# Attends of both pairs of heads of a group of queries in one visit of the matrix engine

## The reference

```python
proj = jnp.einsum('bld,dn->bln', x, w_in) + b_in
qa, fa, ia, za, qb, kb, vb, zb, qi, ki, wi, ga, gb = jnp.split(proj, cuts, axis=-1)
oa = hgrn2_mix(qa, fa, ia, lb)                      # branch A: gated linear recurrence, 4 heads
ob = dsa_mix(qb, kb, vb, qi, ki, wi, rel_bias)      # branch B: attention over chosen keys, 8 heads of 64
...
merged = jax.nn.sigmoid(ga) * ua + jax.nn.sigmoid(gb) * ub
y = jnp.einsum('bld,de->ble', merged, w_out)
return layer_norm(ALPHA * x + y, ln_g, ln_b)
```

```python
logits = jnp.einsum('bthd,btkhd->bhtk', qh, ks).astype(f32) * (HEAD_DIM_B ** -0.5)
logits = logits + bias.transpose(0, 3, 1, 2)
logits = jnp.where(valid[:, None], logits, -jnp.inf)
p = jax.nn.softmax(logits, axis=-1)
o = jnp.einsum('bhtk,btkhd->bthd', p.astype(vs.dtype), vs)
```

## Time and profile before

| | |
|---|---|
| median of 3 runs | 471.39 us (471.04 to 473.29) |
| the profiled execution's own time | 471.07 us |
| its span, first to last instruction | 469.3 us |
| TensorE busy, share | 458.8 us, 98% |
| VectorE, ScalarE, GpSimd busy | 281.2, 217.5, 162.2 us |
| granted TensorE clock, mean | 0.997 of full speed |
| records on TensorE | 2970 matmuls |
| attends (line 635) | 160 records, 12.3 us busy |
| transposes of turns (line 620) | 80 records, 12.1 us busy |

### The profile page before, as it was taken

The page is one execution under the profiler, slowest core; times in us unless marked ns, Lnnn a source line. Parts: engine busy times, 40 slices in busy tenths (PEclk is TensorE's granted clock), DMA queues, the critical chain, the costliest instruction groups (busy, mean ns, idle before and its releaser), DMA issues.

```text
span 469.3 us, 7633 instructions
## 1 busy us (share of the span) xinstructions
PE 458.8 (98%) x2970; PEld 362.9 (77%) x2970; DVE 281.2 (60%) x542; ACT 217.5 (46%) x369; POOL 162.2 (35%) x161
## 2 busy tenths in 40 slices
PE   8999999999999999999999899999999999999994
PEld 7778888888777777666887687787888888888883
DVE  4446589999994243334999984972442332562286
ACT  5635454341336444274966656825872233342000
POOL 0444442491249722582004000000044444994000
PEclk9999999999999999999999999999999999999998
DMA  8818112243022410202022220222033332275022
GB/s 270 271 40 291 57 63 91 89 162 108 0 91 91 125 56 1 91 0 91 3 95 84 91 92 2 92 91 91 0 108 125 106 111 89 91 234 215 0 89 91
DMA packets 15876, 45.64 MB, mean 97 GB/s; under 512 B 2232, under 2 KB 3808, under 8 KB 15840
## 3 DMA queue, kind: packets, MB, share of 16 engines
q1 hardware_dynamic: 15600, 44.96, 28.4%
q10 hardware_dynamic: 240, 0.20, 0.1%
HBM read 43.04 MB, written 2.11 MB: 96 GB/s over the span
## 4 chain that ended last, share of the span: by engine, by line
PE 91%; DVE 5%; issue 2%; DMA 1%; ACT 1%; DVEq 0%; SPq 0%; ACTq 0%
PE bank L479 25%; PE bank L481 24%; PE bank L480 24%; PE bank L611 3%; PE bank L620 2%; PE bank L635 2%; PE bank L707 2%; PE bank L682 2%; DMA w_raw<-in_w_units 1%; PE bank L600 1%; PE bank L601 1%; DVE w_lo L1399 1%; PE bank L525 1%; PE bank L521 1%; PE bank L693 1%
## 5 line engine op out<-in xcount | busy, mean ns | idle before, releaser
L1570 POOL TENSOR_TENSOR w_lo<-w_raw,w_hi 128x512 fp32r<-128x512 f32 x92 | 120.8, 1343 | 167.6 <-ACT w_hi L792 160.9
L479 PE MATMUL bank<-x_hi,w_hi 128*128 128x512 f32 x336 | 134.6, 401 | 0.0
L480 PE MATMUL bank<-x_lo,w_hi 128*128 128x512 f32 x336 | 131.1, 390 | 0.0
L481 PE MATMUL bank<-x_hi,w_lo 128*128 128x512 f32 x336 | 131.1, 390 | 0.0
L479 PEld LDWEIGHTS bank<-x_hi,w_hi 128*128 128x128 f32 x336 | 63.0, 188 | 18.1 <-issue 5.5
L481 PEld LDWEIGHTS bank<-x_hi,w_lo 128*128 128x128 f32 x336 | 63.1, 188 | 13.8
L480 PEld LDWEIGHTS bank<-x_lo,w_hi 128*128 128x128 f32 x336 | 63.2, 188 | 12.1
L792 ACT ACTIVATE w_hi<-w_raw 128x1024 fp32r<-128x1024 f32 (+1 forms) x66 | 66.6, 1027 | 10.9 <-PE bank L481 5.5
L877 ACT ACTIVATE prob<-prob,nmax 128x128 f32<-128x128 f32 (+3 forms) x32 | 17.8, 556 | 49.7 <-DVE nmax L1230 49.6
L1218 DVE COPY prob_t<-bank 128x128 f32<-128x128 f32 (+3 forms) x32 | 14.2, 484 | 33.6 <-PE bank L620 33.6
L1206 DVE MAX8 best<-score 128x8 f32<-128x256 f32 (+2 forms) x48 | 26.8, 558 | 1.0
(11 more groups left out here) (199 smaller groups left out, 718.8 us busy)
## 6 DMA issues: line engine op xcount, KB each, us to landing
w_raw<-in_w_units SPq DMA_DIRECT2D x66, 512.0 KB, 4.6
out<-y_sb SPq DMA_DIRECT2D x8, 256.0 KB, 2.0
x_raw_hi<-in_x_t SPq DMA_DIRECT2D x4, 256.0 KB, 5.7
w_raw<-in_w_units SPq DMA_DIRECT2D x4, 256.0 KB, 5.9
x_raw_lo<-in_x_t SPq DMA_DIRECT2D x4, 256.0 KB, 6.0
t_turned<-t_row SPq DMA_DIRECT2D x1, 1024.0 KB, 9.8
x_res_hi<-in_x_tok SPq DMA_DIRECT2D x2, 512.0 KB, 5.2
x_res_lo<-in_x_tok SPq DMA_DIRECT2D x2, 512.0 KB, 6.8
```

Of the source, the lines that this page charges most:

```text
L479: nc.tensor.matmul(dst, a_hi, b_hi, start=first, stop=False)
L480: nc.tensor.matmul(dst, a_hi, b_lo, start=False, stop=False)
L481: return nc.tensor.matmul(dst, a_lo, b_hi, start=False, stop=last)
L1570: nc.gpsimd.tensor_tensor(split_target(u, kiwi_lo, x_lo, w_lo)[:, k, :], raw(u)[:, k, :], split_target(u, kiwi_hi, x_hi, w_hi)[:, k, :].bi ...
```

## The change

One table is computed differently. `Q_ATTEND`, the quarter of each item's attend, was `Q_ITEM` plus 4 (plus 3 in the second half). Now every item of a group takes the value of the group's last item, so both pairs attend in the quarter in which the second did, the first pair ahead of the second.

```diff
-Q_ATTEND = [Q_ITEM[i] + (4 if i < 16 else 3) for i in range(len(ITEMS))]
+Q_ATTEND = [Q_ITEM[4 * (i // 4) + 3] + (4 if i < 16 else 3) for i in range(len(ITEMS))]
```

## The result

The median of seven runs fell from 471.39 to 468.91 us; the ratio of the runs is 0.9942, with an interval of 0.9927 to 0.9957. The prediction was 469.6, within 0.5% of before, in a range of 468.7 to 471.2. The time lies in the range, but it is 2.48 us under before, where I had forecast 1.82 and had put 0.67 on a difference within 0.5%; faster by more than that had 0.27. Two of the seven runs of before took 473.3 us, and four of 55 later runs of the two kernels were as much longer, at a granted clock of 0.992 or 0.993 in place of 0.995 to 0.998; without the two the median of before is 471.34.

The account below looks back on a forecast made before the run. TensorE, busy 458.8 of 469.3 us, was taken as the bound. Groups 0 to 6 save 6 x 0.29 + 0.15 = 1.89, less 0.07 = 1.82 us: 471.39 to 469.57, say 469.6; range 468.7 to 471.2.

Parts of the forecast that it names:

- The price of an attend: On TensorE, 0.055 us a record plus 0.15 fixed; moving one from ahead of a turn saves 0.29 us.
- The unknown seam between two attends: TensorE's cost between two attends in a row, which the trace didn't show: bounds 0 to 0.15 us, taken as 0.
- Rival B: Every attend pays 0.15 us for each pair, not for the change of kind: 470.6 us; chance 15%.
- Quarter 45: The turn there would wait for its pair's second normalisation on ScalarE; 0.07 us charged against the gain.
- The second place: TensorE meets VectorE's chain at 259.17 us; only the last scores' earlier arrival counts, 1.82 us.
- the stop: TensorE halts 1.47 us in quarter 77, amid 64 small matmuls, with no releaser shown; read as instruction supply running dry.
- the last group: Quarters 66 and 67: its 0.29 us saving lies beside VectorE's chain and only lengthens TensorE's wait at 259 us.
- Behind 259: After 259 us on the timeline TensorE leads and everything else follows its quarters, so the 1.82 us saving stays.
- rival C: Instruction supply runs dry in merged visits' long runs of short matmuls; two stalls give 472.5 us; 9% for two or more.

Follow-up runs that it names:

- the attends apart: The changed kernel with the second pair's attend moved behind the turn in merged visits; 470.60 us, ratio 0.9984 to the kernel before.
- the load held: Kernel before and changed kernel, each with unit 21's weight load delayed until quarter 77's 64 small matmuls finish: 469.67 and 467.73 us; timed again 469.36 and 467.73.
- the three later comparisons: Changed kernel against the kernel before: twice both with unit 21's weight load delayed, 1.94 and 1.63 us less; once both without that delay, 1.95 us less.
- the last group alone: The kernel before with only the last group's attends (quarters 66 and 67) put together: 471.07 against 471.37 us, ratio 0.9993.

## Why the prediction was right, and where it was wrong

**The price of an attend, right.** 0.055 us a record and 0.15 a change of kind hold for 8 to 32 records in a row. The unknown seam between two attends, for which I took 0 of 0 to 0.15, is 0. Rival B falls by the profile and by the attends apart. The cost counts the changes of kind, and neither the pairs nor the visits. With the rule of the Trainium skill, "TensorEngine Tiling (Array Packing)", Key Properties, that a change of tiling mode drains the engine and a change of tile doesn't, the trace agrees: 0.14 to 0.17 us for each change of mode, nothing between the pairs. One reading for the 0 was faulty: 0.85 us for 8 transposes and 0.59 for 4 don't show one pace, since projection follows the first and scores follow the second. With scores behind both it is 1.03 (quarter 53 of before) and 0.59, 0.11 us a transpose.

**Quarter 45, right.** The turn with its wait for the second normalisation takes 0.69 us where four transposes take 0.59: 0.10 lost, where I charged 0.07.

**The second place, right.** The gain that counts at 259 is that of the last scores: 1.82 by the sum, 1.81 to 1.86 in the profiles, 1.63 and 1.94 between pairs of timed kernels without the stop. That the last group earns nothing was shown by doing it alone. I had the place of its wait as L959 "or a little at the tree's first level"; it is all at the first level.

**Behind 259, wrong.** The step that failed is "Behind 259 TensorE leads and everything else follows its quarters, so the 1.82 stays". I had the row of the stop and took its 1.47 us for a constant of the kernel; I used it only as the price of rival C, and put its change at nothing. It is 0.93, 1.45 and 1.56 us in three profiles of the changed kernel, and 0.92 to 1.74 us over eight profiles of five kernels: 0.92 and 0.93 where the instruction packet gets ahead of the end of the weight load, 1.45 to 1.74 where it comes behind the whole load or all but its last packet. A term of plus or minus half a microsecond belongs in a forecast that stands 0.5 us from the bound between the same and faster. Of the 2.5 us between the first two spans it made 0.54. How many of the other timed runs had the short stop is not on record, so what made the first medians 2.48 us apart, 0.66 more than the forecast, is not shown beyond that one pair. In the three later comparisons the change is worth 1.63, 1.94 and 1.95 us, 0.35 to 0.41%; the forecast was 1.82, 0.39%. So the mechanism and its size hold, and the step is the term left out.

**Rival C, half right.** Instruction supply does stop TensorE (1.47 us before, gone with the load held), but no new stop came: 32 short records in a row run through in every profile of the changed kernel.

**Open.** Of the four profiles with groups 0 to 6 together and the load in its place, one has the short stop; of the two of before, none; of the other kernels, the last group alone has it. Whether the change makes the short stop more frequent is not settled by so few; the kernel before showed 1.47 and 1.46 us only. That the packet holds instructions of TensorE is inferred from the stop and the hold, since the profile doesn't name its engine.

## What to carry to other kernels

On a matrix engine that never waits, sort the small work by kind: count the changes of tile shape in a visit, give each its cost from the trace (0.15 us here), and put like with like, with the kind of the surrounding stream at the edge. Then follow the gain to the next place where another engine meets this one, and count only what the last input of that engine gains. A stop to which the profile gives no releaser may be an instruction packet queued behind a large load; compare its time with the transfers, and profile two executions, before it is taken for a constant.

## What the hardware showed that was not expected

- VectorE's 128x1024 difference of two tensors takes 1.22 us alone and 2.20 us with GpSimd's on two tensors beside it, and GpSimd's piece 1.8 us in place of 1.3. Work moved to the idle engine made the chain 1.0 us longer.
